# A chained two-block network on one core: the opening rearranged (bias rows by one product, the first slab alone, later loads held back, x scaled early, constants moved)

## The reference, cut to what matters

```python
def modulate(h, shift, scale):
    return h * (1 + scale[:, None, :]) + shift[:, None, :]

def first_block(x, c, ...):
    cs = silu(c)                                   # (1, 1024)
    for l in range(2):
        if l == 1:
            kv_mod = cs @ kv_mod_w + kv_mod_b      # (1, 2048)
            kv = shared_kv(x, kv_mod[:, :D], kv_mod[:, D:], kv_norm, w_kv)
        mod = cs @ mod_w[l] + mod_b[l]             # (1, 6144): six rows of 1024
        h = modulate(rmsnorm(x, norm_mix[l]), sh_m, sc_m)
        mix = rglru_mixer(h, ...) if l == 0 else moba_mixer(h, ..., rel_bias)
        x = x + g_m * mix
        h = modulate(rmsnorm(x, norm_ffn[l]), sh_f, sc_f)
        x = x + g_f * swiglu(h, ...)
    return rmsnorm(x, final_norm)
```

## Time and profile before

| what | value |
|---|---|
| median of three runs | 1841.08 us (1835.86 to 1845.5) |
| the profiled execution's own time | 1842.03 us |
| its span in the trace | 1840.4 us |
| mean granted TensorE clock, share of full speed | 0.973 |
| busy share: PE, PEld, DVE, ACT, POOL | 94%, 87%, 66%, 49%, 7% |
| bytes read from HBM | 349.45 MB, 192 GB/s over the span |

### The profile page before, as it was taken

The page is one execution under the profiler, slowest core; times in us unless marked ns, Lnnn a source line. Parts: engine busy times, 40 slices in busy tenths (PEclk is TensorE's granted clock), DMA queues, the critical chain, the costliest instruction groups (busy, mean ns, idle before and its releaser), DMA issues.

```text
span 1840.4 us, 29946 instructions
## 1 busy us (share of the span) xinstructions
PE 1734.6 (94%) x11826; PEld 1595.6 (87%) x11826; DVE 1216.6 (66%) x1599; ACT 896.8 (49%) x1235; POOL 122.2 (7%) x163
## 2 busy tenths in 40 slices
PE   6987899999899999999998999988999999999996
PEld 4986799989799998999896899978999896799986
DVE  7889787777765546555676665556655676765556
ACT  4572433356544335434476544345433557644345
POOL 2023111111010000000011000000000003000000
PEclk9998899999999999999999999998999999999999
DMA  9775598868345453555340555434555532355551
GB/s 380 280 292 182 209 358 315 308 232 312 144 172 206 182 183 134 199 193 189 136 178 10 184 200 187 177 138 148 196 193 182 172 138 69 126 184 185 180 197 42
DMA packets 61924, 353.79 MB, mean 192 GB/s; under 512 B 6522, under 2 KB 9738, under 8 KB 27792
## 3 DMA queue, kind: packets, MB, share of 16 engines
q1 hardware_dynamic: 40064, 281.24, 42.2%
q0 software_dynamic: 18384, 66.66, 10.1%
q10 hardware_dynamic: 3392, 4.72, 0.8%
HBM read 349.45 MB, written 3.15 MB: 192 GB/s over the span
## 4 chain that ended last, share of the span: by engine, by line
PE 78%; DVE 11%; ACT 4%; issue 3%; DMA 3%; POOL 0%; DVEq 0%; ACTq 0%; POOLq 0%
PE bank L528 23%; PE bank L529 23%; PE bank L530 23%; DVE w_lo L1509 2%; ACT w_hi L1021 2%; PE bank L560 1%; PE bank L562 1%; PE bank L561 1%; DMA shared<-in_mods 1%; PE bank L700 1%; DVE shared L1530 1%; PE bank L721 1%; DVE shared L2046 1%; PE bank L710 1%; DVE x L2055 1%
## 5 line engine op out<-in xcount | busy, mean ns | idle before, releaser
L528 PE MATMUL bank<-a_hi,w_hi 128*128 128x256 f32 x2648 | 758.8, 287 | 11.0 <-DVE a_lo L1577 3.6
L529 PE MATMUL bank<-a_lo,w_hi 128*128 128x256 f32 x2648 | 754.6, 285 | 0.0
L530 PE MATMUL bank<-a_hi,w_lo 128*128 128x256 f32 x2648 | 754.5, 285 | 0.0
L528 PEld LDWEIGHTS bank<-a_hi,w_hi 128*128 128x128 f32 x2648 | 513.9, 194 | 17.8 <-issue 11.5
L529 PEld LDWEIGHTS bank<-a_lo,w_hi 128*128 128x128 f32 x2648 | 514.0, 194 | 2.9 <-issue 0.7
L530 PEld LDWEIGHTS bank<-a_hi,w_lo 128*128 128x128 f32 x2648 | 513.5, 194 | 0.0
L1771 DVE TENSOR_TENSOR w_lo<-raw,w_hi 128x2048 fp32r<-128x2048 f32 x144 | 330.0, 2292 | 258.2 <-ACT w_hi L1162 258.2
L1162 ACT CAST w_hi<-raw 128x2048 fp32r<-128x2048 f32 x144 | 273.9, 1903 | 268.9 <-PE bank L530 268.9
L1509 DVE TENSOR_TENSOR w_lo<-raw,w_hi 128x2048 fp32r<-128x2048 f32 x119 | 272.1, 2292 | 133.5 <-ACT w_hi L1021 133.4
L1021 ACT CAST w_hi<-raw 128x2048 fp32r<-128x2048 f32 x122 | 231.3, 1907 | 90.9 <-PE bank L530 84.4
L528 PE MATMUL bank<-w_hi,hid_hi 128*128 128x512 f32 x548 | 215.8, 394 | 4.8 <-DVE hid_lo L2192 3.0
(11 more groups left out here) (242 smaller groups left out, 1948.8 us busy)
## 6 DMA issues: line engine op xcount, KB each, us to landing
raw<-in_stream SPq DMA_DIRECT2D x266, 1024.0 KB, 4.8
shared<-in_mods POOLq DMA_DIRECT2D x102, 512.0 KB, 6.3
grow<-in_rows POOLq DMA_DIRECT2D x12, 512.0 KB, 4.0
work<-in_mods POOLq DMA_DIRECT2D x8, 512.0 KB, 9.7
bias_rows<-work ACTq DMA_DIRECT2D x1, 2048.0 KB, 19.0
x<-in_x_t SPq DMA_DIRECT2D x1, 1024.0 KB, 6.2
x<-in_x_d ACTq DMA_DIRECT2D x1, 1024.0 KB, 4.9
work<-bias_rows ACTq DMA_DIRECT2D x1, 1024.0 KB, 10.5
```

What stands on the lines that cost most here:

```text
L528: pe.matmul(out, w_h, v_h, start=start, stop=False, skip_group_check=True)
L529: pe.matmul(out, w_h, v_l, start=False, stop=False, skip_group_check=True)
L530: return pe.matmul(out, w_l, v_h, start=False, stop=stop, skip_group_check=True)
```

## The change

- The bias rows come from one product whose weights are the 33 x 8 table itself; `bias_rows` lies on 8 partitions instead of 128, ACT copies it once, and the store to DRAM repeats each of the 8 rows 128 times in its source pattern. DVE's copy of the table over 128 columns goes; the row of ones is set in the table.
- SP loads slab 0 after 6 conditioning halves, slab 1 after 11 and slab 2 after 14, instead of all three after 9. POOL holds halves 16 to 19 (of the next group) until all 16 of G_MIX0 are added.
- DVE starts with the conditioning halves; the root comes after the eighth half, slab 0's remainder after the fourteenth. x is divided by its root mean square in one instruction of 128 x 2048 behind the last half, into `sq`. The constants from lambda move behind slab 2's remainder.
- ACT makes scale times x plus shift and the rounded high part, in pairs of chunks (`affine_pair`), DVE only the low part (`affine_low`); slab 1's remainder comes after the low parts. ACT rounds slab 2 after the chunks.
- PE takes slab 0 by itself, then slab 1; the ones matrix in every `mod_reduce` has 32 columns instead of up to 128; 4 idle-filling products instead of 9 stand ahead of slab 0.

```diff
@@ -87,7 +87,7 @@
 
 
 OTHERS = (LA_PRE1, LA_PREMIX, LA_PRE2, LA_PREPLE)
-TURNED_CHUNKS = [CH, 0, 0, 0, 0] + [0 if k in OTHERS else APPLY_CHUNKS[5 + k] for k in range(8)] * LAYERS2
+TURNED_CHUNKS = [0, 0, 0, 0, 0] + [0 if k in OTHERS else APPLY_CHUNKS[5 + k] for k in range(8)] * LAYERS2
 
 
 U_LRU, U_FFN0, U_MOBA, U_FFN1 = range(4)
@@ -225,8 +225,7 @@
         mod_more = area(0, 2, 2048)
         mod_third = area(6400, 2048)
 
-        rbb = area(5120, HEADS, P)
-        bias_rows = area(6144, HEADS, 512)
+        bias_rows = area(6144, 512)
         onehot_sb = area(10240, 512)
 
         f_one = area(4096, 2, D)
@@ -274,7 +273,7 @@
         rope_r = xp_all[:, 0:4 * S].rearrange("p (k s) -> p k s", k=4)
         eps = sb("eps", [P, 1])
         warm = sb("warm", [P, 1])
-        rb_sb = sb("rb_sb", [32, HEADS])
+        rb_sb = sb("rb_sb", [33, HEADS])
 
         def col(name, k):
             return cols[:, COL_AT[name] + k:COL_AT[name] + k + 1]
@@ -307,7 +306,8 @@
         silu_done, hid_done, hh_ready, hl_ready = sem("silu_done"), sem("hid_done"), sem("hid_hi_ready"), sem("hid_lo_ready")
         const_ready = sem("const_ready")
         ident0 = sem("ident_zeroed")
-        rbb_ready = sem("rbb_ready")
+        rbb_ready = sem("mask_row_set")
+        xr_ready = sem("x_over_rms_ready")
         row_mm, row_ev = sem("bias_row_made"), sem("bias_row_copied")
         cs_ready = sem("cs_ready")
         mod_step, modc_ready = sem("mod_step"), sem("modc_ready")
@@ -393,8 +393,8 @@
             sp.dma_start(cols[:, :], cols_d).then_inc(s_cols, 16)
             sp.dma_start(x[:, :, :], x_t.rearrange("(c p) s -> p c s", p=P)).then_inc(s_x, 16)
 
-            sp.wait_ge(mod_step, 9)
             for s in range(RING):
+                sp.wait_ge(mod_step, (6, 11, 14)[s])
                 sp.dma_start(raw[:, s, :], stream[s]).then_inc(landed[s], 16)
             with sp.Fori(1, SLABS // RING) as i:
                 for r in range(RING):
@@ -419,7 +419,7 @@
             def mod_half(u):
                 return mods[u // 2][:, u % 2 * MOD_HALF:(u % 2 + 1) * MOD_HALF]
 
-            pool.dma_start(rb_sb[:, :], rb_t).then_inc(s_rb, 16)
+            pool.dma_start(rb_sb[0:32, :], rb_t).then_inc(s_rb, 16)
             pool.dma_start(onehot_sb[0:33, :], onehot).then_inc(s_oh, 16)
             for u in range(2 * MOD_RING):
                 pool.dma_start(mod_slots[u], mod_half(u)).then_inc(mod_landed[u], 16)
@@ -432,7 +432,7 @@
 
             for u in range(2 * MOD_RING, 5 * MOD_RING):
                 slot, _ = mod_slot(u)
-                pool.wait_ge(mod_step, u - 2 * MOD_RING + 1)
+                pool.wait_ge(mod_step, u - 2 * MOD_RING + 1 if u < 4 * MOD_RING else 4 * MOD_RING)
                 pool.dma_start(mod_slots[slot], mod_half(u)).then_inc(mod_landed[slot], 16)
             def mod_loads(lo, hi):
                 with pool.Fori(lo // MOD_RING, hi // MOD_RING) as i:
@@ -642,7 +642,7 @@
                 pe.wait_ge(mod_step, MOD_LAST[g])
                 for m in columns:
 
-                    n = min(P, 512 - m * 32)
+                    n = 32
                     mm = pe.matmul(bank[b][:, m * 32:m * 32 + n], mod_sums(g)[:, m * P:(m + 1) * P], ones[:, 0:n],
                                    start=True, stop=True)
                 mm.then_inc(mod_cols, 1)
@@ -734,25 +734,23 @@
 
 
             pe.wait_ge(const_ready, 1)
-            pe.wait_ge(rbb_ready, 2)
+            pe.wait_ge(rbb_ready, 1)
+            pe.wait_ge(s_rb, 16)
             pe.wait_ge(s_oh, 16)
-            for h in range(HEADS):
-                if h >= 2:
-
-                    pe.wait_ge(row_ev, h - 1)
-                pe.matmul(bank[h % 2][:, :], rbb[0:33, h, :], onehot_sb[0:33, :], start=True, stop=True).then_inc(row_mm, 1)
+            pe.matmul(bank[0][0:HEADS, :], rb_sb[:, :], onehot_sb[0:33, :], start=True, stop=True).then_inc(row_mm, 1)
             norm_stat(N_MIX0)
 
-            pe.wait_ge(row_ev, HEADS)
+            pe.wait_ge(row_ev, 1)
             pe.wait_ge(mod_step, 14)
             keep_warm(8)
             mod_reduce(G_MIX0, 7)
 
 
             need_slab(B_WIN)
-            keep_warm(9)
+            keep_warm(4)
+            feature_slab(B_WIN, bank[0], before(APPLY_CHUNKS, A_MIX0)).then_inc(slab_done, 1)
             need_slab(B_WIN + 1)
-            slab_pair((B_WIN, B_WIN + 1), (bank[0], bank[1]), before(APPLY_CHUNKS, A_MIX0))
+            feature_slab(B_WIN + 1, bank[1]).then_inc(slab_done, 1)
             for i in range(2, 10):
                 s = B_WIN + i
                 need_slab(s)
@@ -1204,13 +1202,16 @@
             act.wait_ge(eps_ready, 1)
             act.wait_ge(s_x, 16)
             squares(N_MIX0, lambda c: x_in[:, c, :], lambda c: None)
-            for h in range(HEADS):
-                act.wait_ge(row_mm, h + 1)
-                act.copy(bias_rows[:, h, :], bank[h % 2][:, :]).then_inc(row_ev, 1)
+            act.wait_ge(row_mm, 1)
+            act.copy(bias_rows[0:HEADS, :], bank[0][0:HEADS, :]).then_inc(row_ev, 1)
             rsqrt(N_MIX0, D)
+            split_to(2)
+            act.wait_ge(xr_ready, 1)
+            act.wait_ge(scale_ready, 1)
+            for b4 in range(4):
+                affine_pair(A_MIX0, b4, lambda m: sq[:, 2 * b4 + m, :], lambda c: scale1[:, c:c + 1], lambda c: modcol(G_MIX0, c))
+            act.dma_start(x[:, :, :], x_d.rearrange("(t p) d -> p t d", p=P)).then_inc(x_landed, 16)
             split_to(RING)
-            normed_hi(A_MIX0, a_out, lambda c: modcol(G_MIX0, c))
-            act.dma_start(x[:, :, :], x_d.rearrange("(t p) d -> p t d", p=P)).then_inc(x_landed, 16)
 
 
             for i in range(5):
@@ -1219,8 +1220,8 @@
                 if i == 0:
                     act.wait_ge(pad_zero, 1)
                 if i == 2:
-                    act.wait_ge(row_ev, HEADS)
-                    act.dma_start(scratch.rearrange("h p s -> p h s"), bias_rows).then_inc(s_rows, 16)
+                    act.wait_ge(row_ev, 1)
+                    act.dma_start(scratch, bias_rows[0:HEADS, :].unsqueeze(1).to_broadcast([HEADS, P, 512])).then_inc(s_rows, 16)
                 if i >= 2:
                     act.wait_ge(conv_done, i - 1)
                 sums = bank[i % 4]
@@ -1832,11 +1833,22 @@
                 split_to(b + 3 * j + 5)
 
 
-            dve.wait_ge(s_rb, 16)
-            dve.tensor_copy(rbb[0:32, :, :], rb_sb[:, :].unsqueeze(2).to_broadcast([32, HEADS, P])).then_inc(rbb_ready, 1)
-            dve.memset(rbb[32:33, :, :], 1.0).then_inc(rbb_ready, 1)
+            dve.memset(rb_sb[32:33, :], 1.0).then_inc(rbb_ready, 1)
             dve.memset(xp[:, :, :, 0:3], 0.0).then_inc(pad_zero, 1)
 
+            dve.wait_ge(cs_ready, 1)
+            for kc in range(8):
+                mod(G_MIX0, kc)
+                if kc == 3:
+                    root(N_MIX0, D)
+                if kc == 6:
+                    split_to(1)
+            dve.tensor_tensor(sq[:, :, :], x_in, rstd[:, N_MIX0 % 2, :].unsqueeze(1).to_broadcast([P, CH, S]), ALU.mult).then_inc(xr_ready, 1)
+            mod_columns(G_MIX0, 7)
+            scale_of(0, G_MIX0, CH, COL_AT["norm_mix"])
+            affine_low(A_MIX0)
+            split_to(2)
+            split_to(RING)
             dve.wait_ge(lam_act, 2)
             lam_n = [0]
 
@@ -1859,17 +1871,6 @@
             lam_link(dve.scalar_tensor_tensor(out=v, in0=v, scalar=2.0, in1=lam[:, 5, :], op0=ALU.mult, op1=ALU.add))
             lam_link(dve.tensor_scalar(lam[:, 7, :], v, 8.0, None, ALU.mult))
             assert lam_n[0] == LAM_STEPS
-            dve.wait_ge(cs_ready, 1)
-            for kc in range(8):
-                mod(G_MIX0, kc)
-            root(N_MIX0, D)
-            split_to(1)
-            mod_columns(G_MIX0, 7)
-            scale_of(0, G_MIX0, CH, COL_AT["norm_mix"])
-            split_to(2)
-            dve.wait_ge(scale_ready, 1)
-            normed(A_MIX0, N_MIX0, x_src, lambda c: scale1[:, c:c + 1], a_h, a_l, lambda c: modcol(G_MIX0, c))
-            split_to(RING)
 
 
             for i in range(5):
@@ -2232,7 +2233,7 @@
 
 def affine_at(ap):
 
-    return CH * (ap - A_FFN0)
+    return CH * ap
 
 
 def rope_slot(h):
```

## The result

The changed kernel takes **1854.78 us** (median of 7 runs, 1850.77 to 1860.38) beside 1838.41 for the kernel before in the same series (7 runs). The ratio is 1.0084, 95% interval 1.0069 to 1.0099: **slower by 0.7 to 1.0%**, some 16 us. The range of the prediction ended at 1851.

What follows compares the result with a forecast made beforehand. PE was taken to bound the kernel, with 78% of the chain. First product -2.0, later mod_reduce -2.0 and +0.5, store +2.5 gave -1.0 against 1842.0, so 1841.0, median 1840; own range 1835 to 1846, wider 1833 to 1851.

Steps and rivals of the forecast that it cites:

- The store: Store of the bias rows, read from 8 partitions while DMA engines are full: +2.5 us, between bounds 0 and 5.1.
- the sum: All terms over the whole kernel added together: -1.0 us against the profiled execution's 1842.0.
- Rival 2: Store of the bias rows: half of the engines carry it in full, +5.1, about 1843 us; chance 0.18.
- Rival 3: Store outlasts its 46 us of cover, ACT waits for it ahead of the gates: 1855 to 1885; chance 0.13.
- The last half's landing: Opening: the last conditioning half lands 1.3 us later, with slabs 0 and 1 ahead of it.
- mod_reduce: Opening: the sums with 32 columns take 3.9 us at half clock instead of 5.39, 1.5 saved.
- -2.0: Two later mod_reduce calls on the chain get shorter with 32 columns: -2.0 us together.
- +0.5: Other later mod_reduce calls, shorter, may leave PE at low clock longer: +0.5 us, from -0.3 to +3.
- From there to the first product: Opening, from the end of mod_reduce to PE's first product: 2.4 us instead of 4.2, 1.8 saved.
- Slabs 0 to 9: First product to slab 9's result: 59.4 us stay within 0.3, with a PE wait of about 1.2 between slabs.
- The held-back loads cost nothing: Opening: holding back the next group's conditioning halves costs nothing, as the first is used at 66.19 us.

Runs made afterwards that it cites:

- fix: The changed kernel with the table spread over 128 columns, 16 per head, so bias rows lie on and are stored from all 128 partitions: 1842.23 us, 1.0019.
- afterwide: The changed kernel with up to 128 columns of ones again, its store still read from 8 partitions: 1854.46 us, 1.0093.
- fixwide: fix with up to 128 columns of ones again, as in the kernel before: 1837.51 us, 0.9993.
- p16: The changed kernel with sixteen bias rows on partitions 0 to 15, two per head: 1845.38 us, 1.0041.
- p8w: The changed kernel with its eight bias rows on partitions 0, 4, ..., 28 instead of 0 to 7: 1840.76 us, 1.0012.
- Fixlate: fixwarm with slab 1 loaded after 14 conditioning halves, slab 2 after 16, and ACT rounding slab 1 behind the chunks: 1842.58 us, 1.0024.
- fixwarm: fix with 54 further idle-filling products on PE between the sum of squares and the wait for the fourteenth half: 1843.73 us, 1.0019.
- best1: fixwide with slab 0's remainder behind x over its root, and slabs 1 and 2 released after 13 and 16 halves: 1835.00 us, 0.9988.
- best2: best1 with the store of the bias rows issued one round of the convolution earlier: 1835.46 us, 0.9989.

## Why the prediction was wrong, step by step

**The store: the step that failed.** It stood at +2.5, from bounds 0 and 5.1. It cost 15.7 us in the traces, 12 us by the ratios (changed kernel against fix) or 18 (afterwide against fixwide). The upper bound charged half of the engines with the store's bytes at the rate of all others. Nothing held that rate fixed: the engine time was 189 us on some 8 engines, 24 us each, where before 91 us lay on 16, 5.7 each. The bound was no bound. Even the engine time is not the price. In p16 the store held 245 us of it (26.4% of the engines for 58 us) and cost only 0.22% against fix, 4 us, since it was over by 90 us; in the changed kernel it slowed the loads issued beside it until 116.7, so that PE ran dry twice. What was missing from the sum is the lateness of those loads.

**Rival 2** (half of the engines, 1843) had the number of engines about right, but that is not what costs: p8w, with eight rows too, can't be told from fix.

So the rule on the slowest dimension in the Trainium skill's page "DMA: Bandwidth & Descriptors" (why a DMA increments its semaphore by 16) fits the 7.3 and 14.7 engines held, but by itself it is not what cost the time.

**Rival 3** came nearest: its 1855 is the result. Its cause, 8 neighbouring partitions at a low rate (I had 52 GB/s alone; 49 were measured beside other loads), is right, though the working is not: 8 of 128 partitions are a sixteenth, 26 GB/s, and no row gave the eighth that I took. Its place is wrong. ACT did not wait for the store ahead of the gates: the slabs came late first, and so the gates were later than the store. By rival 3's own rule, each us beyond 46, the measured store (issued at 62.16, over at about 117, 55 us) would have cost 9 us and given 1850. That its number came out is luck. I had asked only who waits for the store, not who shares its engines. At 0.13 it was given too little.

By Door 1, the port swizzle, in the Trainium skill's page "SBUF — State Buffer", partitions 0 to 7 reach two of 16 ports. The trace agrees in kind: p8w, whose rows lie four partitions apart, does not have the long packets, p16 on partitions 0 to 15 has, and two of 16 ports, the eighth of rival 3, would at the 412 GB/s of the earlier trace rows be 52 GB/s, near the 49 and 50 measured (an estimate). No run counts the ports.

**The last half's landing**: forecast at about 33.3, measured 33.37. Right, and for the reason given: by then the engines had moved 31.4 us x 394 GB/s = 12.4 MB, forecast 12.2. Fixlate adds that behind it DVE's own order is next.

**mod_reduce**: forecast 3.9 us at half clock, measured 5.89 against 5.39 before. That the clock would be low was foreseen (its mean was 0.61 from 34.7 to 40.6 us), the size was not: I had given a narrow pass 0.065 us, by taking a keep_warm price for 26 wide passes off a mixed row and laying the rest on six narrow ones. A pass takes 0.109 us at full clock at any of these widths, so the term is 0, not -1.5, and the later **-2.0** on the chain is 0 too, beside 2 to 5 us lost by the clock (I had +0.5, with +3 as bound).

**From there to the first product**: 2.4 us forecast; 43.01 less 40.60 is 2.4. Right. The forecast of 41 for the first product fails on mod_reduce alone.

**Slabs 0 to 9**: up to 62 us as told. Slab 1's remainder follows the low parts from 48.00, as told. PE had no wait between the slabs where I had 1.2 us, because the low clock lasted to 46.2 us and slab 0 took 7.3 us in place of 6. The recurrence constants held up nothing. What came behind, 59.4 us +-0.3, was 68.8 (43.01 to slab 9's result at 111.78), by the store; in fix it was 59.9, in fixwide 59.5.

**The held-back loads cost nothing**: right; DVE waits for halves 2.9 us from 60 to 130 us in fix, beside 2.2 before.

The store is not the only step that failed. With the store at 0, the sum is -3.5 us, and the kernel to hold beside it is fix, which has the narrow products: it measured 1.0019, +3.5 us. The 7 us between them are, as far as the runs tell, the narrow products: -1.5 and -2.0 that did not come, and 3 to 5 us by the clock in place of 0.5. That fixwide lies about 1 us below the kernel before, as the sum of -1.0 says, is chance.

## What to carry to other kernels

Before a DMA's source is shrunk to a few partitions, ask where they lie: eight rows four partitions apart cost no more time than 128, though the store itself took longer; eight or sixteen neighbouring ones made each packet take up to 3.4 times as long. Ask at what rate such a transfer will run and so how long it lasts, and look for the loss at the loads that are issued meanwhile, not only at whoever waits for the transfer. And fewer columns need not shorten a product: look for rows at both widths first. (That the load of the weights sets the time here fits the equal times; no run tests it.)

## What was not expected of the hardware

- **A transfer can fill the engines without moving much.** With sixteen neighbouring partitions as its source the store held 92% of all 16 engines at 102 GB/s, and three slabs issued in those 12 us, in which no other queue moved a byte, landed after 20.4 us. A high DMA share with low GB/s, 0.88 with 233, is how it shows in a view of stretches.
- **Eight neighbouring partitions hold the loads back while engines stand idle.** From 84 to 93 us the changed kernel's engines were busy for 0.53 of the time and PE for 2.46 of 9 us. That fits loads that are late on the half of the engines that the store uses; no view gives times by engine.
- **An fp32 pass with 128x128 weights took 0.106 to 0.109 us with 32 columns as with 128, and the narrow ones still cost.** Behind the narrow sums the fillers ran at 0.50 in seven kernels of seven, behind the wide ones at 1.00 in seven of seven.
- **The clock in the sums themselves is not explained.** They took from 3.66 to 7.04 us. Neither their width, nor the gap ahead of them, nor the fillers before them settles it: afterwide and fixwide are alike in all three, and differ by 1.5 us.

```profile
34.35 3.76 PE L646 MATMUL bank<-ones,shared 128*128 128x128 f32 x32 [1.23 <-DVE shared L1531]
```
```profile
34.50 5.27 PE L647 MATMUL bank<-ones,shared 128*128 128x128 f32 x32 [1.22 <-DVE shared L1531]
```

With gaps of 1.20 and 0.90 us p8w and p16 had 7.04 us, with 12.2 us of fillers and then gaps of 2.35 and 2.44 us fixwarm had 7.03, and best1 and best2, without a gap, had 3.66. A first product that comes a few us earlier in one profile is therefore no proof of a better order.
